# Block 2's layer 0 in two passes, context tokens first in a stretch of their own; the expert layers of block 1 sorted, 28 experts in fours

## What is computed

```python
# block 1: an "even" layer (windowed attention and spatial gating), an "odd" layer (gated short convolution)
for l in (0, 1):
    lat = lat + g1 * mixer_l(modulate(rms_norm(lat)))           # the context tokens only give keys and values, in layer 0
    h2  = modulate(rms_norm(lat))
    lat = lat + g2 * moe_ffn(h2)                                # 4 groups of 8 experts, the best 2 of one group per token
# moe_ffn: for a token and its two experts e: gate_e * ((silu(h @ w_gate[e]) * (h @ w_up[e])) @ w_down[e]), hidden 512
# block 2: x_lat and x_ctx, two layers; a layer is
a   = x * (1 + sc1) + sh1                                       # its own six modulation vectors for latents and context
f, nq, nk, nv, cq, ckv, kr, g = split(a @ w_in)
y   = [fourier_mix(f), neighbourhood_attention(nq, nk, nv, context keys), latent_attention(cq, ckv, kr, context keys)]
m   = sum(sigmoid(g_b) * (y_b @ w_branch_b) for b in 0, 1, 2) @ w_out
x   = layer_norm(ALPHA * x + (1 + g1) * m)
x   = layer_norm(ALPHA * x + (1 + g2) * swiglu(x * (1 + sc2) + sh2))   # hidden 2816
```

## Time and profile before

| | |
|---|---|
| median of 3 runs | 3313.26 us |
| the profiled execution | 3326.3 us |
| its span, first to last instruction | 3324.5 us |
| mean granted TensorE clock | 0.961 |
| busy: TensorE, VectorE, ScalarE | 3126.6, 921.6, 512.8 us |
| moved | 688.35 MB, mean 207 GB/s |
| busy TensorE of the chain that ended last | 90% |

### The profile page before, as it was taken

One profiled execution on the slowest core, in us unless ns is written; L12 is line 12 of the kernel. 1 busy time (PEld: TensorE's weight loads), 2 busy tenths in 40 slices (PEclk: granted clock), 3 DMA queues, 4 the chain that ended last, 5 costly groups with the idle time before them and its releaser, 6 DMA issues.

```text
span 3324.5 us, 32506 instructions
## 1 busy us (share of the span) xinstructions
PE 3126.6 (94%) x12888; PEld 1744.3 (52%) x12888; DVE 921.6 (28%) x2176; ACT 512.8 (15%) x1022; POOL 0.2 (0%) x4
## 2 busy tenths in 40 slices
PE   6998999998989999979988999999999899799998
PEld 3565444446754444434534444344444355487886
DVE  2332212222122222240437343352221213512002
ACT  1121111111021111120424000010000013301000
POOL 0000000000000000000000000000000000000000
PEclk8888999999989999989999999999999999899999
DMA  8616999996769999921110333133332131133440
GB/s 368 266 74 261 425 429 429 428 429 250 282 242 427 427 429 428 428 117 60 42 51 26 152 127 126 51 127 152 145 142 93 51 127 51 51 127 127 152 152 13
DMA packets 49553, 688.35 MB, mean 207 GB/s; under 512 B 5296, under 2 KB 7344, under 8 KB 7728
## 3 DMA queue, kind: packets, MB, share of 16 engines
q1 hardware_dynamic: 47696, 680.55, 50.1%
q10 hardware_dynamic: 1760, 6.43, 0.5%
HBM read 685.91 MB, written 1.05 MB: 207 GB/s over the span
## 4 chain that ended last, share of the span: by engine, by line
PE 90%; DVE 6%; issue 2%; DMA 1%; ACT 1%; ACTq 0%; SPq 0%; DVEq 0%
PE bank L360 61%; PE bank L591 23%; PE bank L427 2%; PE bank L454 1%; DMA ring<-in_stream 1%; PE bank L445 1%; DVE X L1274 1%; DVE work L1160 1%; DVE work L1054 1%; DVE MX L1115 1%; DVE work L1133 0%; PE bank L616 0%; ACT work L854 0%; PE bank L633 0%; DVE work L1100 0%
## 5 line engine op out<-in xcount | busy, mean ns | idle before, releaser
L360 PE MATMUL bank<-A,ring 128*128 128x256 f32 (+1 forms) x3088 | 1001.5, 484 | 23.3 <-issue 13.3
L360 PEld LDWEIGHTS bank<-A,ring 128*128 128x128 f32 x3088 | 592.9, 193 | 405.4 <-issue 345.4
L591 PE MATMUL bank<-ring,work 128*64 128x512 f32 x3072 | 673.3, 594 | 2.7 <-ACT work L940 2.7
L360 PE MATMUL bank<-work,ring 128*128 128x256 f32 (+1 forms) x1696 | 538.2, 475 | 12.3 <-DVE work L1061 8.2
L360 PEld LDWEIGHTS bank<-work,ring 128*128 128x128 f32 x1696 | 324.1, 192 | 216.3 <-issue 175.3
L591 PEld LDWEIGHTS bank<-ring,work 128*64 128x64 f32 x3072 | 217.1, 137 | 411.8 <-issue 407.9
L360 PE MATMUL bank<-work 128*128 128x128 f32 (+3 forms) x2016 | 264.9, 310 | 15.0 <-DVE work L1263 10.0
L360 PEld LDWEIGHTS bank<-work 128*128 128x128 f32 (+2 forms) x2016 | 195.4, 177 | 41.3 <-issue 36.4
L1160 DVE SCALAR_TENSOR_TENSOR work<-ring,SILC,work 128x512 f32<-128x512 f32 x224 | 154.4, 747 | 2.0
L360 PE MATMUL bank<-ring,A 128*128 128x512 f32 (+1 forms) x320 | 122.4, 543 | 13.7 <-issue 12.3
L591 PE MATMUL bank<-work 128*128 128x256 f32 x512 | 127.7, 392 | 3.4
(11 more groups left out here) (181 smaller groups left out, 1677.4 us busy)
## 6 DMA issues: line engine op xcount, KB each, us to landing
ring<-in_stream SPq DMA_DIRECT2D x324, 2048.0 KB, 12.3
X<-in_xt ACTq DMA_DIRECT2D x1, 2048.0 KB, 18.6
tab_sb<-in_tab_a ACTq DMA_DIRECT2D x1, 1120.0 KB, 25.8
X<-in_ctx2t ACTq DMA_DIRECT2D x1, 1024.0 KB, 8.1
out<-X SPq DMA_DIRECT2D x1, 1024.0 KB, 4.8
tab_sb<-in_tab_b ACTq DMA_DIRECT2D x1, 960.0 KB, 4.7
par_sb<-in_par ACTq DMA_DIRECT2D x1, 618.0 KB, 9.3
work<-in_wsp ACTq DMA_DIRECT2D x1, 512.0 KB, 31.4
```

Source lines behind the costliest of these rows:

```text
L360: m = pe.matmul(o, w, x, start=start, stop=stop, tile_position=place)
L591: m = pe.matmul(o, w, x, start=start, stop=stop)
```

## The change

Three parts.

Experts. After routing, VectorE sorts the experts by their number of tokens and writes the order as integers; experts 0 and 1 always come first. SyncE reads the order from SBUF into registers and issues strips by it. The first four places run as pairs with 64 rows each, the other 28 in seven units of four with 32 rows each. Each unit's four gate strips come together, then four up, then four down; the ring still has six slots. The hardware loop is gone. If an expert outside the first four has over 32 tokens, or one of them over 64, the further passes run.

Context. The context half of layer 0 is written as a generator on TensorE, ScalarE and VectorE. Each `yield` on TensorE carries a cost, and `beside(slot, us)` runs steps until a budget is used up. In expert stage 0 there are 5 us of budget per unit; everything else has budget 0 up to `beside("rest", 1e9)`, which stands after ln_in. Its weights are fetched again, by POOL's queue, as 182 quarters of a strip (0.52 MB each) into a ring of four of its own; the first 48 are layer 0's twelve modulation strips. It uses two banks and one probability buffer for a pair of heads. Keys and values of the context are written to DRAM and read back for the latents.

Latents. Layer 0 then runs as layer 1 does, 256 columns wide. The odd layer has four modulation strips fewer, the merge has none; layer 1's twelve stay in layer 0's up products.

```diff
+HOT, HOT_C, COLD_C = 4, 64, 32
+UNITS = HOT // 2 + (EXPERTS - HOT) // 4
-    ("moe0", 3 * EXPERTS), ("odd", 20), ("moe1", 3 * EXPERTS),
-    ("l0_na", 4), ("l0_bias", 1), ("l0_low", 1), ("l0_up", 1), ("l0_merge", 17), ("l0_out", 2), ("l0_ffn", 29),
+    ("moe0", 3 * EXPERTS), ("odd", 16), ("moe1", 3 * EXPERTS),
+    ("l0_na", 4), ("l0_bias", 1), ("l0_low", 1), ("l0_up", 1), ("l0_merge", 9), ("l0_out", 2), ("l0_ffn", 29),
...
+QTILES, QRING = 8, 4
+QUARTERS = [(FIRST["l0_mods"] + n, q) for n in range(12) for q in range(4)]
+for _stage, _tiles in (("l0_na", 128), ("l0_low", 32), ("l0_up", 28), ("l0_merge", 288), ("l0_out", 64), ("l0_ffn", 528)):
+    QUARTERS += [(places(_stage, "E")[t // TILES], t % TILES // QTILES) for t in range(0, _tiles, QTILES)]
...
+            def experts(l):
+                first = FIRST[f"moe{l}"]
+                s = first
+                for u, (at, n, _) in enumerate(units()):
+                    if u == 1:
+                        sp.wait_ge(order_ready, l + 1)
+                    ids = [sp.value_load(ORDI[0:1, l, at + i:at + i + 1], min_val=0, max_val=EXPERTS - 1) if u else at + i
+                           for i in range(n)]
+                    for m in range(3):
+                        for e in ids:
+                            sp.wait_ge(strip_used, s - RING + 1)
+                            sp.dma_start(ring[:, s % RING, :], stream[e * 3 + (first + m)]).then_inc(strip_in[s % RING], 16)
+                            s += 1
...
+        @block.gpsimd
+        def _(pool):
+            last_taken(pool, "even_out")
+            pool.dma_start(cTAB, tab_b[:, 0:1280]).then_inc(c_tab_in, 16)
+            for m, (s, q) in enumerate(QUARTERS):
+                if m >= QRING:
+                    pool.wait_ge(c_used, m - QRING + 1)
+                n = QTILES * P
+                pool.dma_start(cring[:, m % QRING, :], stream[s][:, q * n:(q + 1) * n]).then_inc(c_in[m % QRING], 16)
...
+            def unit(l, u):
+                U = l * UNITS + u
+                at, n, c = units()[u]
+                first = FIRST[f"moe{l}"] + 3 * at
+                pace = (0, 1.5, 1.5, 2) if l == 0 else (0, 0, 0, 0)
+                def product(half, ready):
+                    for k in range(KD):
+                        for e in range(n):
+                            W = strip(first + half * n + e)
+                            m = mm(bank[half][e * c:(e + 1) * c, :], XG(k)[:, e * c:(e + 1) * c], W[:, k * HID:(k + 1) * HID],
+                                   k == 0, k == KD - 1, tells=k == KD - 1 and e == n - 1, place=(0, e * c) if c == 32 else None)
+                            if k == KD - 1:
+                                used()
+                    m.then_inc(ready, 1)
...
+                product(0, gate_ready)
+                beside(f"a{U}", pace[0])
+                product(1, up_ready)
+                beside(f"b{U}", pace[1])
+                pe.wait_ge(hid_ready, U + 1)
...
+                    gather(gath_ready)
+                beside(f"c{U}", pace[2])
+                pe.wait_ge(he_ready, U + 1)
...
+                beside(f"d{U}", pace[3])
...
+                link(dve.scalar_tensor_tensor(KEY, MS, float(EXPERTS), par_("keyoff"), ALU.mult, ALU.add))
+                link(dve.tensor_tensor(G3, rowed(KEY), lined(KEY), ALU.is_gt))
+                link(dve.reduce_sum(POS, G3, AXX))
+                link(dve.tensor_tensor(G3, rowed(POS), lined(par_("expert")), ALU.is_equal))
+                link(dve.tensor_tensor(G3, G3, rowed(par_("expert")), ALU.mult))
+                link(dve.reduce_sum(ORD, G3, AXX))
+                dve.tensor_copy(ORDI[:, l, :], ORD).then_inc(order_ready, 1)
...
-            norm("ln_in", 2 * T, mean=True)
+            norm("ln_in", T, mean=True)
+            beside("rest", 1e9)
             for l in range(2):
-                w = streams(l)
+                w, kw = T, KEYS[l]
...
-                            if l == 0 and at // TILES < 8:
-                                reduce_mod(MERGE_MOD + at // TILES)
...
+                    for k in range(KD):
+                        dve.tensor_scalar(A[:, k, T:2 * T], X[:, k, T:2 * T], MODP[:, 1, 8 + k, 1:2], MOD[:, 3, k, 1:2],
+                                          ALU.mult, ALU.add).then_inc(ctx_a_ready, 1)
```

One step of the context's attention on TensorE, for a pair of heads e:

```diff
+                    for t in range(n + 2):
+                        if t >= 2:
+                            wait_ctx(pe, "turn", name, t - 2)
+                            b, r = cgroup("pv", name, t - 2), rows(t - 2)
...
+                        if 1 <= t <= n:
+                            pe.wait_ge(c_pn, u0 + t)
+                            b = cgroup("turn", name, t - 1)
+                            for j in range(4):
+                                m = turn(b[:, j * P:(j + 1) * P], cPR[:, j // 2, (j % 2) * P:(j % 2 + 1) * P], tells=j == 3)
+                            m.then_inc(c_lin, 1)
+                        if t < n:
+                            b = cgroup("s", name, t)
+                            for e in range(2):
+                                m = mm(b[:, e * T:(e + 1) * T], q(t, e), key(t, e), True, True, tells=e == 1)
+                            m.then_inc(c_lin, 1)
+                        yield 3.5
```

More of the change, by code:

```diff
@@ L68 @@
 EVEN_OUT_MOD, ODD_MOD = len(MODS) - 3, len(MODS)
[L69 to L77, removed]
+MODS += [(s, 1, 16 + 4 * i, 1) for i, s in enumerate(places("odd", "M"))]
 FFN_MOD = len(MODS)
@@ L84, in sum_rows @@
     rows = lambda m: [2 * (m % 2), 2 * (m % 2) + 1] if MODS[m][3] == 2 else [m % 4]
-    before = [m + 1 for m in range(MERGE_MOD, n) if set(rows(m)) & set(rows(n))]
+    before = [m + 1 for m in range(FFN_MOD, n) if set(rows(m)) & set(rows(n))]
     return rows(n), max(before, default=0)
[L89 to L100, removed]
-            (f"mv{_l}", "DDDD"), (f"qrope{_l}", "D" * 8),
-            (f"merge{_l}", "ADADAD" * KD), (f"out{_l}", "D" * KD), (f"up{_l}", "AD" * KF), (f"down{_l}", "D" * KD)]
-GROUP0, TAKER, TAKEN = {}, [], []
@@ L146 @@
     ("gq", 4), ("gkv", 2), ("sink", HEADS), ("rbias", 2 * TB * ROUTES),
-    ("ident", P), ("ones", P), ("before", P), ("expert", EXPERTS), ("group", EXPERTS), ("slot", C), ("cond", 2),
+    ("ident", P), ("ones", P), ("before", P), ("expert", EXPERTS), ("group", EXPERTS), ("slot", C), ("cond", 2), ("keyoff", EXPERTS), ("slots", UNITS), ("iota", P),
 ])
@@ L384, in mod_rows, with beside @@
+            thread = context()
+            due = [0.0]
+            def beside(slot, us):
+                due[0] += us
+                n = 0
+                while due[0] > 0:
+                    cost = next(thread, None)
+                    if cost is None:
+                        break
+                    due[0] -= cost
+                    n += 1
+                SPLIT[slot] = n
             def mod_rows(n):
@@ L959, in moe @@
                        .then_inc(taken["A"], 1)
+                beside(f"turn{l}")
                 act.wait_ge(rt_exp_in, l + 1)
@@ L1356, in moe @@
+                wait_taken(dve, f"rows{l}", 1)
+                for u in range(UNITS):
+                    unit(l, u, g2)
+                dve.wait_ge(res_added, 4 * UNITS * (l + 1))
                 dve.wait_ge(flag_ready, l + 1)
@@ L1564, in lay_out @@
         put(None, [sets[which][chunk // 4]], s)
+    for i in range(12):
+        put(None, [sets[2][i]], FIRST["l0_mods"] + i)
     w = I["w_in_even"][0]
```

1183 lines of the change are left out of this document (936 added, 247 removed).

## The result

The changed kernel takes **3569.5 us** (median of 4 runs, 3554.5 to 3588.5) against 3309.4 (4 runs): ratio 1.080, 95% interval 1.076 to 1.083. The forecast was 3600, between 3480 and 3735.

A forecast was written before the change was run, and what follows sets the result against it. Each expert stage was taken as bound equally by TensorE and transfers (29.3 and 29.4 us per pair). 3326 + 76 + 102 + 125 - 12 - 8 + 3 = 3612, less 13: 3600 us, range 3480 to 3735.

The forecast's parts named there:

- Bounds of the kernel before: Expert stages: TensorE at 29.3 us per pair and transfers at 29.4 us, two bounds of the same size.
- the rival that transfers follow TensorE: Expert stages: 428 GB/s is TensorE's pace, not a ceiling, so fours shorten a stage; some 3070 us at best, chance 0.05.
- Fours: Expert stages: groups of four break the strips' stream at a lowered clock, period 22.9 us, 538 us against 475, +63 us.
- The rival of the whole stream: Expert stages: the strips' stream stays unbroken, groups take 19.6 to 20.6 us, total say 3520 us; chance 0.25.
- Quarters: First expert stage: 48 modulation quarters, 59 us of transfers, partly fill stream breaks; net +26 us, bounds +15 and +59.
- ride in TensorE's idle time: First expert stage: the context steps placed there, 5 us of budget per unit, use time when TensorE is idle.
- Sort: Ahead of each expert stage's first gather: sorting experts stands on the path, +13 us per stage.
- Context stretch: Between the expert stages, all on the path: products 468, attention 130, norms 62, ramps and waits 20, sum 680 us.
- the rival of POOL's queue: Quarters on POOL's queue come late; at 4.5 us per issue they cost 143 us, total 3740 us; chance 0.15.
- Layer 0's latents: Block 2, layer 0 with latents alone: 622 us; with the context stretch 1302 against 1177, +125 us.
- Small ones: Odd mixer -12 us, ln_in half as wide -8, context modulation for layer 1 on VectorE +3.
- The odd mixer: Odd mixer: four fewer weight sets at about 3 us each, -12 us.

The follow-up runs named there:

- pairs: Changed kernel with all experts of both stages in pairs of 64 rows, no fours, and smaller modulation steps: 3503.2 us, ratio 1.054.
- halves: Changed kernel with each product of a unit of four done as two halves, experts 0 and 1 first, then 2 and 3: 3507.4 us.
- the dummy products: Changed kernel with unread extra products in the second expert stage's units of four, to keep TensorE's clock up: 3546.2 us.
- the same with them moved: Changed kernel with the context's 12 modulation strips taken out of the first expert stage and put between it and the odd mixer: 3614.0 us.
- the best variant: Changed kernel, context spread over both expert stages, modulation handed out more slowly, products of the first stage's first two fours in halves: 3193.5 us, ratio 0.963.
- even modulation: Changed kernel with the first expert stage's modulation steps handed out evenly, 1.25 us at each of a unit's four steps: 3581.6 us.
- the first spread: Changed kernel with the context stretch spread over both expert stages, 10 us a step in all fours: 3213.8 us, ratio 0.968 to the kernel before.

## Why the forecast came out, and where its steps were off

**Bounds of the kernel before.** Right: half the gate and up products leave the stage within 8 us, so the rival that transfers follow TensorE falls.

**Fours.** The mechanism was right and is shown by pairs, by halves and by the dummy products; the size was too large. The period was put at 22.9 us and is 21.8, the product at 9.6 us and averages 9.1. 20 groups x 1.1 = 22 us are most of the 28 by which +63 missed. (The four losses at the half clock average 2.4 us, not 2.3. The 7.3 us for a product at full clock stood below the 8.1 of its row, 64 x 0.127, without a reason given; it measured 7.05.) The rival of the whole stream (19.6 to 20.6 us a group) is wrong, but it is what the order of two halves gives.

**Quarters.** This step failed in its reasoning. "They fill breaks in the other stream in part", net +26; they cost 70 us (580.3 - 510.1 by the second stage, and the same with them moved), above the bound of 59. The breaks were not filled on balance: 224.2 MB in the first stage and 194.9 in the second are 524 and 455 us at 428 GB/s, so the engines miss some 56 us of the one and 55 of the other. (Of the 29 MB between them 25.2 are the quarters, the rest strips of the ring that still land in the longer stage.) Of the 56, some 10 are the stop of the stream in the first pair. That is also what the prediction's "ride in TensorE's idle time" has wrong: the steps stand in TensorE's order, and while it waits in one it holds the ring's slots. The error of this step (44 us too little) went against that of the group's period (28 too much, in each stage), and the sum of the stages, +152 forecast, came to +141. That the total fell so near is in this part luck.

**Sort.** +8.9 and +8.6 for +13: from the rank's product to the first expert product 23.2 and 22.8 us after, 14.2 before.

**Context stretch.** 644 us for 680. The norms were right (23.8 and 20.2 us for 24 and 20). The eight attention steps of the first round take 6.0 us each, as taken (5.9); here are the turns of two steps:

```profile
1681.65 1.11 PE L540 MATMUL bank<-par_sb,work 128*128 128x128 f32 x4 [0.99 <-DVE work L1768]
...
1687.66 1.11 PE L540 MATMUL bank<-par_sb,work 128*128 128x128 f32 x4 [0.99 <-DVE work L1768]
```

The eight of the other two rounds take 4.5 to 6.1 us, and the six ramp steps, priced in full (35 us), are short. From first scores to last product the three rounds take about 50, 24 and 23 us, 97 for the 130 forecast and under its bound of 105 (22 x 4.7 is 103, by the way); that is nearly all of the miss. In the view of waits for this stretch the chain through VectorE stands first, and the quarters have one wait of 0.4 us:

```profile
PE bank L540 <- DVE work L1768: 25.3, 16, 3.3
PE bank L536 <- DVE work L1708: 16.9, 2, 8.5
...
PE bank L536 <- DMA work<-in_stream: 0.4, 1, 0.4
```

So the rival of POOL's queue is wrong here: 4.3 us to landing in this stretch for the 3.9 assumed. The Trainium skill ("DMA: Bandwidth & Descriptors", SWDGE vs HWDGE vs iDMA) warned of VectorE locking POOL out; with VectorE busy 124 of 644 us no row of this trace shows it. The queue was late in two other places, beside the strips (16.1 us to landing) and alone with TensorE (6.3 us), and there it cost.

**Layer 0's latents.** 634.8 for 622, layer 1 662.8 for 647.5. Nearly all of this is the clock in the attention (last section), which other variants with the same instructions there do not pay. The attention of layer 1 before, and of layer 0's latents after, with the low-rank products between its rounds:

```profile
2759.50:2903.00 143.50, 124.84 (x606) 72.40 (x606) 70.86 (x179) 53.66 (x121) 0.00 (x0) 0.92 0.16 59
...
2316.60:2460.30 143.70, 126.48 (x603) 78.36 (x602) 65.90 (x177) 52.48 (x122) 1.33 (x2) 0.82 0.20 68
```

The second has 12 us less to do by the forecast (low, mk and mv) and takes as long, at 0.82 for 0.92: these 12 are the 12.8 that were missing. Layer 1's attention took 17 us more than before, at 0.82 too, and the layer 15.

**Small ones.** The odd mixer gave 5.1 us for 12; why less was not looked into.

## What to carry over

Where two bounds are equal, making one cheaper gains nothing, and how the cheaper form holds its buffers can break the other: four strips needed at once on six slots broke a stream that a loop order of two at a time leaves whole. Freed time of an engine is worth something only where that engine's other work is put into it; the change paid for the fours and for the stretch but left them apart, and handing the one to the other's idle time turned +8.0% into -3.2% (-3.7% in the best variant). Where transfers are the bound, a second queue's bytes cost at least their own time: 59 us of bytes cost 70 us beside fours and 86 beside halves, part of it because TensorE waited for them while it held the first queue's slots.

## What the runs showed beside that

The clock in the attention has two courses for the same instructions. Layer 1's attention took 160.2 us at a mean clock of 0.82 in the kernel after (the last two rows of its stretches above), and in the kernel with the lowest time:

```profile
2628.50:2770.50 142.00, 123.42 (x607) 70.95 (x606) 70.94 (x179) 53.92 (x121) 0.00 (x0) 0.94 0.17 60
```

607 instructions in both; 34.1 us at 0.50 (1.2 GHz) at its start in the one, full clock (2.4 GHz) there in the other, and 18 us between them. Of the profiles of the changed kernel and its variants, four (the changed kernel, pairs, halves, even modulation) have the longer course in layer 1, seven the shorter, with the kernel before. Block 1's attention does the same: 42.9 us from first turn to last in the kernel after for 56.6 before, which is the -17.6 us of the account but for 4. In layer 0's latents the attention took 146 us in the same four profiles and 130 to 142 in the seven. What decides it was not found; no edit here was made for it. It may be the cause of runs of one kernel in groups (3202.3, 3202.4, 3225.2, 3225.3 of the first spread), which no trace of the unprofiled ones can show.
